# Cache pages laid four tokens to a partition instead of one

## The reference

```python
k_past = cache_k[i, page_table].reshape(DB, past_len, DIFF_HEADS, 2, DIFF_DH)
v_past = cache_v[i, page_table].reshape(DB, past_len, DIFF_HEADS, DIFF_DV)
...
s_past = jnp.einsum('bqhcd,bkhcd->bhcqk', q, k_past).astype(F32) * scale
s_new = jnp.einsum('bqhcd,bkhcd->bhcqk', q, k).astype(F32) * scale
s_new = jnp.where(jnp.tril(jnp.ones((T, T), dtype=bool)), s_new, -jnp.inf)
a = jax.nn.softmax(jnp.concatenate([s_past, s_new], axis=-1), axis=-1)
w = (a[:, :, 0] - lam * a[:, :, 1]).astype(v.dtype)
return (jnp.einsum('bhqk,bkhv->bqhv', w[..., :P], v_past)
        + jnp.einsum('bhqk,bkhv->bqhv', w[..., P:], v))
```

## Time and profile before

| what | value |
|---|---|
| median of 3 runs | 1885.47 us (1884.6 to 1886.47) |
| span of the profiled execution | 1880.3 us |
| PE busy | 1773.0 us, 94% |
| PEld, DVE, ACT, POOL busy | 87%, 63%, 39%, 18% |
| data moved by DMA | 265.73 MB |
| key and value page transfers | 256 and 256, 256 KB each |
| median from issue to landing | 5.7 us (keys), 5.5 us (values) |
| mean granted TensorE clock | 0.978 |

### The profile page before, as it was taken

How to read it: one execution, slowest core, us unless ns; L and a number is a source line. 1 busy time by engine, 2 the same in 40 slices (tenths; PEclk the granted TensorE clock), 3 DMA queues, 4 the chain that set the end, 5 groups by cost and what they waited for, 6 DMA issues and landing times.

```text
span 1880.3 us, 35481 instructions
## 1 busy us (share of the span) xinstructions
PE 1773.0 (94%) x13062; PEld 1639.1 (87%) x13062; DVE 1192.5 (63%) x1946; ACT 735.6 (39%) x1418; POOL 341.2 (18%) x360
## 2 busy tenths in 40 slices
PE   6999999996999999996999999999999999999998
PEld 6999999984666667665998999999999999999997
DVE  4223742475777777765458876667677878699443
ACT  5113322564655565653225333222323424245320
POOL 1111331001233333332111211211121000000110
PEclk9999999898999999998999999999999999999998
DMA  5323551227999999977111222222222424232121
GB/s 162 108 80 82 141 140 56 61 83 236 330 350 354 346 357 360 353 231 226 35 45 46 80 69 81 81 70 69 81 70 69 157 81 134 74 106 86 47 69 48
DMA packets 232923, 265.73 MB, mean 141 GB/s; under 512 B 16162, under 2 KB 173428, under 8 KB 232756
## 3 DMA queue, kind: packets, MB, share of 16 engines
q1 hardware_dynamic: 211988, 195.36, 33.2%
q0 software_dynamic: 20768, 68.17, 10.7%
HBM read 229.79 MB, written 29.21 MB: 138 GB/s over the span
## 4 chain that ended last, share of the span: by engine, by line
PE 45%; DVE 6%; ACT 1%; issue 1%; DMA 1%; POOL 0%; DVEq 0%; ACTq 0%
PE psum L2518 33%; PE psum L150 10%; DVE x_second_lo L2532 1%; DVE unit_lo L1910 1%; DMA x_first_hi_raw<-scratch_z 1%; PE psum L2197 0%; PE psum L2894 0%; DVE x_second_lo_raw L2536 0%; DVE rstd_and_products L2576 0%; DVE x_first_lo L2532 0%; DVE h L2576 0%; ACT unit_hi L1904 0%; DVE rstd_and_products L2009 0%; DVE x_lo L2226 0%; DMA w_raw<-in_w_ple_gate 0%
## 5 line engine op out<-in xcount | busy, mean ns | idle before, releaser
L2518 PE MATMUL psum<-x_second_hi,unit_hi 128*128 128x364 f32 x924 | 304.5, 330 | 8.0 <-DVE x_second_lo L2532 4.6
L2518 PE MATMUL psum<-x_second_hi,unit_lo 128*128 128x364 f32 x924 | 303.4, 328 | 0.0
L2518 PE MATMUL psum<-x_second_lo,unit_hi 128*128 128x364 f32 x924 | 303.4, 328 | 0.0
L1303 POOL DMA_DIRECT2D dec_v<-in_cache_v x256 | 137.6, 538 | 288.1 <-issue 282.2
L150 PE MATMUL psum<-x_hi,w_hi 128*128 128x364 f32 x768 | 182.0, 345 | 5.8 <-DVE x_lo L2226 5.8
L2518 PEld LDWEIGHTS psum<-x_second_hi,unit_hi 128*128 128x128 f32 x924 | 173.8, 188 | 10.8 <-issue 5.7
L2518 PE MATMUL psum<-x_first_hi,unit_hi 128*128 128x364 f32 x528 | 173.7, 329 | 0.6 <-DVE x_first_lo L2532 0.6
L2518 PEld LDWEIGHTS psum<-x_second_hi,unit_lo 128*128 128x128 f32 x924 | 174.0, 188 | 0.0
L2518 PEld LDWEIGHTS psum<-x_second_lo,unit_hi 128*128 128x128 f32 x924 | 173.7, 188 | 0.0
L2518 PE MATMUL psum<-x_first_hi,unit_lo 128*128 128x364 f32 x528 | 173.5, 329 | 0.0
L2518 PE MATMUL psum<-x_first_lo,unit_hi 128*128 128x364 f32 x528 | 173.2, 328 | 0.0
(11 more groups left out here) (313 smaller groups left out, 3313.3 us busy)
## 6 DMA issues: line engine op xcount, KB each, us to landing
dec_k<-in_cache_k SPq DMA_DIRECT2D x256, 256.0 KB, 5.7
dec_v<-in_cache_v POOLq DMA_DIRECT2D x256, 256.0 KB, 5.5
w_raw<-in_w_in SPq DMA_DIRECT2D x25, 512.0 KB, 3.9
scratch_z<-ffn_hidden SPq DMA_DIRECT2D x22, 546.0 KB, 2.8
w_raw<-in_w_ffn_gate SPq DMA_DIRECT2D x22, 512.0 KB, 3.8
w_raw<-in_w_ffn_up SPq DMA_DIRECT2D x22, 512.0 KB, 3.8
w_raw<-in_w_ffn_down SPq DMA_DIRECT2D x16, 512.0 KB, 4.0
feat_swap<-feat_n SPq DMA_DIRECT2D x32, 136.5 KB, 2.4
```

The costliest lines, as they stand in the source:

```text
L1303: eng.dma_start(ring[:, slot, p:p + 1, :], cache[bass.ds(page, 1)].rearrange("o t f -> t o f")).then_inc(sem, 16)
L2518: ins = pe.matmul(bank[b], w[unit][:, j, :], x[slot][:, j, :], start=start and j == 0 and w is m.uhi and x is m.xhi7, stop=j == k - 1 and ...
```

## The change

A page goes to 32 partitions instead of 128. Page p of a group fills partitions 32p to 32p + 31 of the slot, over all four column blocks: partition 32p + j holds tokens 4j to 4j + 3 of page p, which are 8192 contiguous bytes of the cache. After the four transfers the slot is as full as before. Keys and values go through the same function, so their tokens are in the same new order. Nothing else is edited.

```diff
     for p in range(4):
         page = eng.value_load(ids[0:1, 4 * n + p:4 * n + p + 1], min_val=0, max_val=POOL - 1)
-        eng.dma_start(ring[:, slot, p:p + 1, :], cache[bass.ds(page, 1)].rearrange("o t f -> t o f")).then_inc(sem, 16)
+        eng.dma_start(ring[32 * p:32 * p + 32, slot, :, :], cache[bass.ds(page, 1)].rearrange("o (j r) f -> j (o r) f", r=4)
+                      ).then_inc(sem, 16)
```

## The result

The changed kernel takes 2049.74 us (median of 4 runs, 2044.15 to 2062.97) against 1885.76 us for the kernel before on the same chip: ratio 1.089, 95% interval 1.0867 to 1.0912. It is slower, and close to the 2054 us that were forecast. The profiled execution has a span of 2046.7 us, 166.4 us more than before.

A forecast was written before the change was run, and what follows sets the result against it. TensorE was taken to bound the attention, with DMA just behind. At 235 GB/s its 142.0 MB take 604 us instead of 435, so 1885.5 + 169 = 2054 us; range for 8 in 10: 1920 to 2135 us.

The forecast's parts named there:

- Who paces the stage: Attention: TensorE sets the pace at 6.25 us a step, with the DMA engines close behind and no idle DMA time.
- 15 us of cover: Attention page rings: pages asked for four steps ahead leave some 15 us spare, a one-off stock that cannot offset a lower rate.
- Longer rows: Attention page loads: 8192-byte rows run between 312 and about 411 GB/s, gaining at most 11 us at the stage's ends.
- Fewer partitions: Page loads: a transfer to 32 partitions reaches eight of 16 SBUF ports and runs at 218 to 225 GB/s, about half.
- the swap: feat_swap, four DMAs to 32 partitions each in the earlier trace: 218 GB/s, taken as the pattern of the changed loader.
- The doubt about the issue: SP issues feat_swap at 222 GB/s, so issuing alone, not the few partitions, could explain its 218 GB/s.
- Two queues at once: Attention, keys beside values: two thirds of the bytes at 220 GB/s, one third at 274, 235 in all; +169 us.
- The clock: TensorE in the attention: 9.4 us a step leave room for a mean clock down to about 0.65; nothing added.
- The packets: Sign expected in the attention's profile: fewer DMA packets, of more than double the length per byte.
- rival 1: Attention page loads: longer rows win and 32 partitions cost nothing, 312 to 411 GB/s, 1875 us; chance 7%.
- rivals 2 and 3: Attention queues: either complementing each other (1900 us, 11%) or in lockstep on equal or path-sharing partitions (2140 us, 13%).
- Rival 3: Attention, both queues always on the same or path-sharing partitions: 206 GB/s, +254 us, 2140 us; chance 13%.

The follow-up runs named there:

- the tests: Two blocks of bare transfers, eight cases each, put ahead of the kernel before to measure rates by partitions written: 205 to 427 GB/s.
- the last test: Bare transfers ahead of the kernel before, twelve of 256 KB a queue: SP to 32 partitions as in the change, GpSimd to all 128; 242 to 243 GB/s.
- turning the values: Changed kernel with value pages of a group issued in the order 2, 3, 0, 1, keys as they were: 2053.98 us, ratio 1.0902.
- the pattern 0, 2, 1, 3: Changed kernel with the four pages of a group issued in this order in both queues: 2027.08 us, ratio 1.0783.

## Why the prediction was right

- *Who paces the stage.* Right. TensorE had been the bound with the engines just behind; 15 us of cover were no rate. PE's waits for pages rose by 132 us. (Slices 9 and 18 of the earlier trace rows are at 6 tenths for PE, not 9: they are the ramp and the end, where it waits.)
- *Longer rows.* Its bound of 11 us stands: to all partitions, with one transfer of 1 MB for four, they gave 5 us. The price for row length was too high, though: the 312 GB/s of the earlier trace rows came from 8 us of the ramp, and by themselves 2048-byte rows ran at 389 to 391 GB/s once under way, against 427 for 8192 bytes.
- *Fewer partitions.* Right, and the step that carries all: half the rate, read from 22 packets of x_sample and the swap. Beside their 225 and 218 GB/s the tests have 208 for partitions 0 to 31 and 220 for the four sets in turn; 64 partitions were tried only in the kernel (247 GB/s from both queues). The doubt about the issue is settled for the cache pages: SP issued the twelve transfers of the last test in 5.78 us, 544 GB/s, and such transfers ran at 220 alone. Whether the swap itself was held by its issue stays open; the tests carry the step without it.
- *Two queues at once.* The mean was right, its two parts were not. I had 220 GB/s for two thirds of the bytes and 274 for one third, 235 in all, and 235 is what the stage had. But nothing ran at 274: unlike halves gave 234, queues two pages apart 212, and the same order 240. The assumption that a packet is doubled half of the time and single otherwise is not shown by any run. That the forecast came within 5 us of the measured time is luck in this term: its two wrong parts have the right mean.
- *The clock.* I added nothing for it. PE's granted clock was 0.88 for most of the stage, and PE was busy 45.3 us longer for the same 13062 matmuls (1818.3 against 1773.0 us). So it was busy 72% of the stage (432 of 602 us), where about 60% was expected. The slower PE took the place of waiting and did not add to the time: the bare transfers, without any matmul, ran at the same 240 GB/s.
- *The packets.* They were to take more than double the time a byte and took 1.5 times. The sign was set too high against the sum beside it: 235 GB/s in place of 344 to 352 is 1.5 times.
- *The rest.* The stages before 434 us and behind the attention kept their length, as said.
- *The rivals.* The gain (rival 1) does not come with this partition set; a fixed relation of the queues (rivals 2 and 3) was excluded by the rate and by turning the values. Rival 3 also had two queues in the same order at 206 GB/s; by themselves they ran at 240.

Shown is that the choice of partitions is the cause: with every fourth partition and all else equal, the loss is gone. Open stays why the pattern 0, 2, 1, 3 is faster in the kernel (256 against 241 GB/s) and slower by itself (223 against 240), and why turning the values costs 12% by itself and next to nothing in the kernel. That engines share paths, and how they drift against each other, is argued here and not shown: the profile does not say which engine a packet ran on.

## What to carry to other kernels

The rate of the transfers here was set by which partitions they write, before their row length: 32 neighbours ran at half rate (208 GB/s against 427), 64 were hardly better in the kernel (247 GB/s against 241), and what ran beside them was slowed too. Where a page must go to fewer than 128 partitions, spread them over all (every fourth), which cost 0.2% here. And before making a transfer more efficient, read whether anyone waits for it: at 6.25 us a step TensorE took next to no gain from it, but had only 5 to 11% of rate to lose.

## What the runs showed of the hardware that was not expected

- Transfers to every fourth partition run at 387 GB/s from one queue and 392 from two, and at 423 once under way: nearly the 427 of all 128.
- Transfers to 32 neighbouring partitions slow the other queue too: together with transfers to all 128 they have 242 to 243 GB/s, where two queues to all 128 had 370.
- Two queues writing unlike halves of the partitions do not add up: 234 GB/s, against 206 on the same half.
- A DMA share of 1.00 to 1.03 was read at 205 GB/s and at 427 GB/s. It does not tell how much room is left.
